# Attention pipeline in a decoder trunk: distance 6 instead of 4, more buffers, and two output weight slots rounded behind the loop

## What is computed

```python
aq, ak, av, iq, ik, iw, pu, mq = jnp.split(h @ w_in[l], IN_OFFSETS, axis=-1)
y_attn = dsa_attention(aq, ak, av, iq, ik, iw)      # 8 heads x 64, top 128 keys of each query
y_pool = multiscale_pool(pu, w_pool[l], scale)      # trailing means
y_mem = memory_attention(mq, mem_n, w_kv, ...)      # 4 heads x 64, into 256 memory tokens
x = x + jnp.concatenate([y_attn, y_pool, y_mem], axis=-1) @ w_out[l]
```

## Time and profile before

| | |
|---|---|
| median of three executions | 1859.08 us (1858.18 to 1864.09) |
| profiled execution, its own time | 1859.6 us |
| span in its profile | 1857.8 us |
| PE busy | 1845.5 us (99%) |
| DVE busy | 1185.5 us |
| ACT busy | 993.7 us |
| POOL busy | 667.5 us |
| attention loop, layer 0 | about 483 to 549 us of the span |
| attention loop, layer 1 | about 1405 to 1471 us |

### The profile page before, as it was taken

The page is one execution under the profiler, slowest core; times in us unless marked ns, Lnnn a source line. Parts: engine busy times, 40 slices in busy tenths (PEclk is TensorE's granted clock), DMA queues, the critical chain, the costliest instruction groups (busy, mean ns, idle before and its releaser), DMA issues. The chain is left out here.

```text
span 1857.8 us, 33596 instructions
## 1 busy us (share of the span) xinstructions
PE 1845.5 (99%) x11685; PEld 1624.9 (87%) x11685; DVE 1185.5 (64%) x1925; ACT 993.7 (53%) x1610; POOL 667.5 (36%) x530
## 2 busy tenths in 40 slices
PE   9999999999999999999999999999999999999999
PEld 7999988887778899998889999888877789999887
DVE  6989821378754998941098998114787459999311
ACT  6444554575656544454474445546657564444642
POOL 2366611112511266631115666111216012666210
DMA  8433398888238633378874334988881485333885
GB/s 230 122 103 100 114 218 190 183 203 199 63 92 192 139 111 102 101 190 195 192 171 114 97 106 124 218 191 202 188 202 34 100 205 128 110 95 112 203 196 133
DMA packets 78087, 277.23 MB, mean 149 GB/s; under 512 B 8624, under 2 KB 10928, under 8 KB 77744
## 3 DMA queue, kind: packets, MB, share of 16 engines
q1 hardware_dynamic: 48960, 175.67, 30.4%
q0 software_dynamic: 28464, 98.05, 29.7%
q10 hardware_dynamic: 576, 2.36, 0.4%
HBM read 175.91 MB, written 2.10 MB: 96 GB/s over the span
## 5 line engine op out<-in xcount | busy, mean ns | idle before, releaser
L560 POOL DMA_DIRECT2D w_lo<-raw x179 | 153.9, 869 | 769.9 <-ACT w_lo L1258 730.8
L632 POOL TENSOR_TENSOR w_lo<-s_sum,w_hi 128x512 fp32r<-128x512 f32 x200 | 318.0, 1604 | 244.0 <-ACT w_hi L1306 244.0
L1257 ACT ACTIVATE w_hi<-raw 128x1024 fp32r<-128x1024 f32 x155 | 164.0, 1058 | 338.3 <-PE bank L688 322.9
L688 PE MATMUL bank<-t_hi,w_hi 128*128 128x256 f32 x1152 | 326.7, 284 | 2.1 <-DVE zf L1787 2.1
L688 PE MATMUL bank<-t_lo,w_hi 128*128 128x256 f32 x1152 | 326.0, 283 | 0.0
L688 PE MATMUL bank<-t_hi,w_lo 128*128 128x256 f32 x1152 | 325.9, 283 | 0.0
L688 PE MATMUL bank<-a_hi,w_hi 128*128 (+1 forms) x832 | 324.6, 390 | 0.0
L688 PE MATMUL bank<-a_lo,w_hi 128*128 (+1 forms) x832 | 323.8, 389 | 0.0
L1306 ACT ACTIVATE w_hi<-s_sum 128x512 fp32r<-128x512 f32 x216 | 127.7, 621 | 275.3 <-DVE s_sum L1769 269.4
L688 PE MATMUL bank<-a_lo,w_lo 128*128 (+1 forms) x704 | 273.9, 389 | 0.0
L1699 DVE TENSOR_TENSOR a_hi<-zf,a_lo (+1 forms) x88 | 64.0, 731 | 322.3 <-ACT a_lo L1366 322.2
(11 more groups left out here) (210 smaller groups left out, 3884.7 us busy)
## 6 DMA issues: line engine op xcount, KB each, us to landing
raw<-weights SPq DMA_DIRECT2D x326, 512.0 KB, 4.2
w_lo<-raw POOLq DMA_DIRECT2D x179, 512.0 KB, 6.2
x<-x_t SPq DMA_DIRECT2D x4, 512.0 KB, 7.1
t_lo<-t_sum POOLq DMA_DIRECT2D x4, 512.0 KB, 6.6
b_lo<-hn POOLq DMA_DIRECT2D x4, 512.0 KB, 7.3
mem<-mem_t ACTq DMA_DIRECT2D x2, 1024.0 KB, 7.1
out_t<-x SPq DMA_DIRECT2D x8, 256.0 KB, 2.1
const<-consts SPq DMA_DIRECT2D x1, 481.5 KB, 9.8
```

The costliest lines, as they stand in the source:

```text
L560: G.dma_start(w_lo[:, s], raw[:, s], accum_op=ALU.add).then_inc(w_ready[pos], 16)
L632: G.tensor_tensor(out=fast_weight(l, e, product, 0, True), in0=s_sum[i - 1][:, :], in1=fast_weight(l, e, product, 0, False).bitcast(f32), ...
L688: return nc.tensor.matmul(out_, lhsT, rhs, start=start, stop=stop, skip_group_check=True)
L1257: nc.scalar.activation(w_hi[:, s], raw[:, s], ACT.Copy).then_inc(w_hi_done, 1)
```

## The change

The distance between logits and transposes (`LAG`) is 6 units instead of 4. There are eight `prob` and eight `pt` tiles instead of four each, and the masked logits go through four tiles instead of two; the waits that protect these tiles reach back accordingly. The added tiles lie in space that is free in this stage. Only slots 0 and 1 of the output projection are rounded within the loop; `round_ahead` behind the loop begins two slots earlier, with slots 2 and 3.

```diff
-LAG = 4
-OUT_ROUND_UNITS = (9, 11, 21, 23)
+LAG = 6
+PT = 8
+AHEAD = 8
+OUT_ROUND_UNITS = (9, 11)
...
-    pt = [place(f"pt{i}", T, h_at + i * tile_b) for i in range(4)]
+    pt = [place(f"pt{i}", T, h_at + (i % 4 + 2 * (i - i % 4)) * tile_b) for i in range(PT)]
...
-           [place(f"prob{i}", T, h_at + (4 + i) * tile_b)[:, :] for i in range(2)]
+           [place(f"prob{i}", T, h_at + (4 + i) * tile_b)[:, :] for i in range(2)] + \
+           [place(f"prob{i}", T, h_at + (10 + i) * tile_b)[:, :] for i in range(2, AHEAD - 2)]
+    logit = [t2[:, 0:T], t2[:, T:2 * T]] + \
+            [place(f"logit{i}", T, a_hi_at + (8 + i) * tile_b)[:, :] for i in range(2)]
...
-        if n >= 4:
-            eng.wait_ge(pv_done[n % 2], l * (UNITS // 2) + (n // 2 - 1))
-        copy(pt[n % 4][:, 0:blocks * P], bank[2 + n % 2][:, 0:blocks * P])\
+        if n >= PT:
+            eng.wait_ge(pv_done[n % 2], l * (UNITS // 2) + ((n - PT) // 2 + 1))
+        copy(pt[n % PT][:, 0:blocks * P], bank[2 + n % 2][:, 0:blocks * P])\
...
-                                                   prob[n % 4][:, b * P:(b + 1) * P], con(C_ID, P))
+                                                   prob[n % AHEAD][:, b * P:(b + 1) * P], con(C_ID, P))
...
-                                      pt[(n + half) % 4][:, b * P:(b + 1) * P], b == 0, b == blocks - 1)
+                                      pt[(n + half) % PT][:, b * P:(b + 1) * P], b == 0, b == blocks - 1)
...
-                    if n >= 4:
-                        act.wait_ge(ptp_done, l * UNITS + (n - 3))
-                    nc.scalar.activation(prob[n % 4][:, 0:blocks * P], chunk(t2, n % 2, T, blocks * P),
+                    if n >= AHEAD:
+                        act.wait_ge(ptp_done, l * UNITS + (n - AHEAD + 1))
+                    nc.scalar.activation(prob[n % AHEAD][:, 0:blocks * P], logit[n % 4][:, 0:blocks * P],
...
-                for k in range(DC - 1):
+                for k in range(len(OUT_ROUND_UNITS) - RING, DC - 1):
                     round_ahead(l, MIX_BASE["out"] + k)
...
-                    if n >= 2:
-                        dve.wait_ge(p_ready, l * UNITS + (n - 1))
+                    if n >= 4:
+                        dve.wait_ge(p_ready, l * UNITS + (n - 3))
                     wait_apart(dve, logit_done[n % 2], l * (UNITS // 2) + (n // 2 + 1))
-                    V.tensor_tensor_reduce(out=chunk(t2, n % 2, T, blocks * P),
+                    V.tensor_tensor_reduce(out=logit[n % 4][:, 0:blocks * P],
```

## The result

The changed kernel takes 1876.47 us (median of four, 1874.77 to 1877.58) against 1859.65 us for the kernel before: a ratio of 1.0089, 95% interval 1.0076 to 1.0102. It is slower, by 16.8 us, and lies above the predicted range, which ended at 1872.5 us. Measured once more beside the kernel before, in a later comparison, it came out at 1874.31 against 1859.76, a ratio of 1.0075 (1.0061 to 1.0088), 14.0 us as ratio times time. A ratio here is the one on record, not the quotient of the two medians beside it, from which it differs by up to 0.0008.

A forecast was written before the change was run, and what follows sets the result against it. PE was taken to bound the kernel, busy 1845.5 of 1857.8 us. A 4.3 us stall less 0.4 us loop gain, in both layers, added 7.8 us: 1866.9 us forecast, range 1862.8 to 1872.5.

The forecast's parts named there:

- The sign: Whole kernel: slower than before, at 0.82; same 0.15, faster 0.03.
- the main term: Behind the attention loop, PE waits at `out_chunk(2)` for late-rounded out slot 3: 4.3 us once per layer.
- the landings right behind it: Slot 4's landing and the raw reloads after slots 3 and 4 arrive before they are needed: no cost.
- the clock behind the stall: Rival, 0.15: after PE's wait for slot 3, TensorE falls to half pace, costing 2.7 us per layer.
- 0.4 us gained per layer: Attention loop: 0.5 + 0.4 + 0.1 us back and 0.6 given, so 0.4 us shorter per layer.
- the late transpose at step 28: Attention loop: the second late transpose, 0.60 us late, gets 0.4 back as two roundings leave the loop.
- The one at step 16: Attention loop: the first late transpose gets 0.5 us back, as `split_y` moves away from an out slot's rounding.
- the second `pool_map`: Attention loop: it needs `over_sums(3)`, now only one PE step earlier; cost 0.3 us, with one `split_y` delaying a copy.
- the end of the loop: Last loop steps: one step more, another change of shape (0.17 us) and less cover for copies (0.1): cost 0.3 us.
- The 0.1 us from four `logit` tiles: Attention loop: DVE's mask waits for an older exponential, n-4 instead of n-2; PE gains 0.1 us per layer.
- The 0.17 us gaps at changes of shape: PE gaps in the loop, taken as the price of changing shape; rival at 0.03: waits for data, giving 1853.9 us.
- The forecast lower bound of the loop: Attention loop if nothing is got back: a loss of 0.7 us.

The follow-up runs named there:

- two `rt` tiles: Changed kernel with the third out slot rounded early, plus a second tile for the spread inverse sums: 1861.98 us, ratio 1.0012 to the kernel before.
- DVE's order was changed: DVE's `split_y` one step later, in the distance 6 kernel with early third slot and second `rt` tile: 1859.33 us, ratio 0.9992 to the kernel before.
- The same edit alone: The kernel before (distance 4, four slots in the loop) with only DVE's `split_y` moved one step later: 1858.95 against 1860.20 us, ratio 0.9993.

## Why the prediction was wrong

The sign was right and the main term was right: the stall was forecast as 4.3 us once per layer and measured as 4.14 and 4.16, with the chain behind it as it was built from the rows. Nothing took it back, and the landings right behind it stayed hidden, as said. Two steps failed: the clock behind the stall, which the sum had at nothing, and the loop, which the sum had as a gain. They cost 3.1 and 4.1 us, the stall was 0.3 us shorter than its term, and that makes the 6.9 us between the 7.8 forecast and the 14.7 of the parts. Added to the forecast of 1866.9 us, either alone would have stayed under the 1872.5 of the range; both, with the shorter stall, give 1873.8.

**The clock.** It was a rival at 0.15, and it happened in both layers of all three profiles in which PE stands idle there, and at this place in none of the others. I had argued against it only that no row shows such a fall, which is no evidence in a trace without such a gap. Behind the wait the matmuls stand 0.43 us apart, at a granted clock of 0.63 and 0.52 in two windows. The Trainium skill, "TensorE: Matmul & The Clock Gate", section "HAM oscillation — how this bites in real kernels", says that PE is throttled again while it waits for the DMA and starts its next burst cold. This case's traces agree in the main. They differ in that in two of the six waits, and in the one of 2.48 us, the first matmuls behind it still stood 0.23 us apart and the slow ones came up to 1 us later. The price was taken from the start of the kernel as 2.7 us per layer and is 1.55 (1.7 by the starts of the matmuls): the slow stretch was about 3.6 us long, not 5.4.

**"0.4 us gained per layer".** It is 1.65 us lost, 4.1 us over both layers. The three gains: the late transpose at step 28 went, as forecast (0.4). The one at step 16, now at step 18, was to give back 0.5 and gave nothing, 0.67 us late instead of 0.62: I had moved `split_y` away from the out slot's rounding without asking what it moves to. It moved onto `copy_rt` of the next group. Moving a stage by two steps on an engine that works in order needs a look at every instruction of the step it lands on; `copy_rt` and its wait for `y_ready` stood in the code. The costs, in layer 0: the first steps 0.37 (0.1 was said), the second `pool_map` 0.33 (0.3 was said: it waited for `over_sums` at 522.11, but no split stood ahead of that), the transpose at step 42 0.92 instead of 0.29 (not foreseen), the end of the loop 0.63 where 0.36 stood, and the changes of shape. The 0.1 us from four `logit` tiles isn't seen: at distance 4 the loops are 65.16 and 65.44 us with the added tiles, 65.21 and 65.37 without.

With two `rt` tiles the transpose at step 42 was still 0.73 us late. That went when DVE's order was changed. The same edit alone, in the kernel before, took 1.3 and 1.2 us off the loops, more than the 1.0 forecast as gains of the whole change: the late copies hung on the place of the split in DVE's list, which the change left as it was. Why step 42 was later than the 0.29 us at distance 4 is only argued: the spreading of the inverse sums, 0.4 us of PE's work, no longer stands in the step between.

**What held.** PE still waits for the copies out of the two transpose banks; the greater distance didn't help there. The 0.17 us gaps at changes of shape are still there, so they are no waits for late data. The forecast lower bound of the loop, a loss of 0.7, was too narrow. The first measurement is 2.1 us above the parts. Its profile has 2.9 us of longer wait and third slow stretch in the kv projection. That its other three executions had the same is likely but not shown: their mean clock is 0.996 or 0.997, where the second measurement has 0.998 in three of five, and by an estimate a stretch of 3.6 us at half clock takes 0.001 off the mean of a span of 1875 us.

## What to carry to other kernels

When a stage is moved in a pipeline of in-order engines, write down the step it lands on, on each engine, with every instruction and wait already there: a single-buffered tile that was two steps away can become the next thing in line. A rounding or a load that feeds the busiest engine through a DMA must be issued a landing plus its own work ahead (here 4.6 us from POOL's issue to PE's start, behind 2.6 us of rounding); a queue that is done "behind the loop" starts only after that engine's last dependent instruction. And a wait of 4 us on TensorE cost more than 4 us here, since the matmuls behind it ran at half pace. Filling the wait with matmuls of no use won back 1.5 us of it per layer; rounding the slot before the wait won back both.

## What the runs showed of the hardware

- A wait of 4.1 to 4.2 us was followed by the 1.2 GHz pace in both layers of each of the three profiles with it: the matmuls stood 0.43 us apart instead of 0.23, for about 3.6 us. In layer 1 of the kernel with two slots in the loop at distance 4, and in layer 0 of the second profile of the changed kernel, the first matmuls behind the wait (from 1480.58 and from 556.20) still ran at full pace.
- Shorter waits were followed by it too. The one of 2.48 us in the kv projection of the first profile was followed by a granted clock of 0.67. At the start of the kernel the clock fell in two profiles (0.57 and 0.59 in the window from 10 to 14 us, with four slots in the loop at distance 6 and in the kernel before with the later split), where PE had stood idle for 2.14 and 2.45 us until ACT's first `h_hi` was ready. In the kernel before it stood idle there for 1.42 us, and the clock stayed at 1.00. These falls come and go with the length of a wait that none of the edits touches.
- The granted clock reads 1.00 over the first twelve matmuls, which go at 0.45 us each; it doesn't show their slow pace.
- In the loops PE's weight loads start 0.17 us late where the shape of the loaded block changes, and 0.36 us behind 512-wide matmuls, at distance 4 and at distance 6 alike.
- The adding DMA of 512 KB into `w_lo`, issued to an idle queue with another 1.9 us behind it, let PE start 4.6 us and SP 4.7 us after POOL issued it, in both layers of all three profiles.
